# A two-block transformer kernel on one core: ring slots, rotations and first scores around its third attention reordered

## The reference, cut to what matters

```
q_l, k_l, v_l = jnp.split(h_lat @ w_in, 3, axis=-1)
q_l = apply_rope(q_l.reshape(B, S, DIFF_HEADS, 2, HEAD_DIM), cos, sin)
k_l = apply_rope(k_l.reshape(B, S, DIFF_HEADS, 2, HEAD_DIM), cos, sin)
k_c, v_c = jnp.split(h_ctx @ w_in[:, DIFF_QK_COLS:], 2, axis=-1)
...
s = jnp.einsum('bqhtd,bkhtd->bthqk', q, k).astype(jnp.float32) * HEAD_DIM ** -0.5
p = jax.nn.softmax(s, axis=-1)
a = (p[:, 0] - lam * p[:, 1]).astype(v.dtype)
o = jnp.einsum('bhqk,bkhe->bqhe', a, v)
```

## Time and profile before

| | |
|---|---|
| Median of 3 runs | 2924.38 us (2922.2 to 2927.43) |
| The profiled execution | 2922.9 us |
| Its span, first to last instruction | 2921.0 us |
| TensorE busy | 2822.2 us, 97% of the span |
| TensorE weight loads | 2314.3 us |
| DVE busy | 1386.3 us |
| ACT busy | 973.7 us |
| Mean granted TensorE clock | 0.985 of full |

### The profile page before, as it was taken

One profiled execution on the slowest core, in us unless ns is written; L12 is line 12 of the kernel. 1 busy time (PEld: TensorE's weight loads), 2 busy tenths in 40 slices (PEclk: granted clock), 3 DMA queues, 4 the chain that ended last, 5 costly groups with the idle time before them and its releaser, 6 DMA issues.

```text
span 2921.0 us, 43108 instructions
## 1 busy us (share of the span) xinstructions
PE 2822.2 (97%) x18438; PEld 2314.3 (79%) x18438; DVE 1386.3 (47%) x2449; ACT 973.7 (33%) x1565; POOL 63.1 (2%) x53
## 2 busy tenths in 40 slices
PE   7999999999999998999999999999998999999999
PEld 5876578888888887876778888887875788788887
DVE  3464553433233334325756646459478433443333
ACT  2144552422112224215635323342146322332221
POOL 2000000100000000000001001100000000000000
PEclk9999999999999999999999999999999999999999
DMA  6232101122332231220011333312220233222322
GB/s 263 87 102 77 36 12 48 58 102 105 116 127 101 103 107 30 65 65 22 1 58 59 101 102 96 99 59 66 87 84 23 65 94 101 87 86 85 104 96 85
DMA packets 67790, 238.53 MB, mean 82 GB/s; under 512 B 7440, under 2 KB 10640, under 8 KB 66960
## 3 DMA queue, kind: packets, MB, share of 16 engines
q1 hardware_dynamic: 67312, 234.20, 24.3%
q10 hardware_dynamic: 288, 1.57, 0.2%
HBM read 233.64 MB, written 2.10 MB: 81 GB/s over the span
## 4 chain that ended last, share of the span: by engine, by line
PE 91%; DVE 6%; ACT 2%; issue 1%; DMA 1%; SPq 0%; DVEq 0%; ACTq 0%
PE PSA L660 88%; PE PSA L966 2%; PE PSA L1246 1%; DVE stat L2988 1%; DVE WS L2213 1%; DMA Y<-in_early 1%; PE PSA L1556 0%; DVE Y L3001 0%; DVE HS L2383 0%; DVE PSA L2987 0%; ACT WS L1646 0%; ACT HS L1733 0%; DVE X L2321 0%; DVE X L2355 0%; ACT Y L1718 0%
## 5 line engine op out<-in xcount | busy, mean ns | idle before, releaser
L660 PE MATMUL PSA<-HS,WS 128*128 128x512 f32 (+1 forms) x6672 | 1349.3, 362 | 19.5 <-DVE HS L2383 12.8
L660 PEld LDWEIGHTS PSA<-HS,WS 128*128 128x128 f32 x6672 | 1124.7, 189 | 231.5 <-issue 30.5
L2213 DVE TENSOR_TENSOR WS<-W,WS 128x1024 fp32r<-128x1024 f32 (+2 forms) x318 | 364.3, 1147 | 610.2 <-ACT WS L1646 609.2
L1646 ACT ACTIVATE WS<-W 128x1024 fp32r<-128x1024 f32 (+2 forms) x318 | 314.1, 989 | 794.2 <-PE PSA L660 420.9
L660 PE MATMUL PSA<-YS,WS 128*128 128x512 f32 (+1 forms) x2232 | 470.2, 372 | 3.6 <-DVE YS L3026 3.6
L660 PEld LDWEIGHTS PSA<-YS,WS 128*128 128x128 f32 x2232 | 392.4, 189 | 79.1 <-DVE YS L3026 4.0
L660 PE MATMUL PSA<-Y 128*64 128x128 f32 (+9 forms) x2368 | 287.6, 345 | 16.6 <-ACT Y L1794 6.1
L660 PEld LDWEIGHTS PSA<-Y 128*64 128x64 f32 (+3 forms) x2368 | 178.5, 156 | 95.5 <-issue 69.2
L1630 ACT ACTIVATE Y<-PSA 128x512 f32<-128x512 f32 (+5 forms) x77 | 53.4, 699 | 243.0 <-PE PSA L660 242.9
L660 PE MATMUL PSA<-HS,YS 128*128 128x512 f32 (+1 forms) x696 | 129.1, 343 | 4.5 <-issue 4.1
L660 PEld LDWEIGHTS PSA<-HS,YS 128*128 128x128 f32 x696 | 108.5, 192 | 21.8 <-issue 7.3
(11 more groups left out here) (332 smaller groups left out, 2295.0 us busy)
## 6 DMA issues: line engine op xcount, KB each, us to landing
W<-in_weights SPq DMA_DIRECT2D x396, 512.0 KB, 3.6
Y<-in_early SPq DMA_DIRECT2D x4, 2048.0 KB, 18.6
W<-in_weights SPq DMA_DIRECT2D x24, 256.0 KB, 2.5
X<-in_x SPq DMA_DIRECT2D x4, 768.0 KB, 20.0
W<-in_weights SPq DMA_DIRECT2D x24, 128.0 KB, 2.1
Y<-in_ssm ACTq DMA_DIRECT2D x1, 1024.0 KB, 6.8
out<-X SPq DMA_DIRECT2D x1, 1024.0 KB, 4.6
C<-in_consts SPq DMA_DIRECT2D x1, 948.5 KB, 30.9
```

Of the source, the lines that this page charges most:

```text
L660: return pe.matmul(out, lhsT, rhs, start=first, stop=last)
L1646: act.activation(split_home(n)[:, 0, 0:f], W[:, c % W_RING, 0:f], ACT.Copy)\
L2213: tt(home[:, 1, 0:f], W[:, c % W_RING, 0:f], home[:, 0, 0:f].bitcast(F32), ALU.subtract)\
```

## The change

Four things, all of them in the order of instructions; no arithmetic is added or removed.

1. `first_tiles_of` (used at all five norms): the wait for the weights and the slot of each of the three tiles stands before that tile's first product, no longer before all three; the second tile goes to slot 2 and the third to slot 1. In DVE's table three residual adds stand earlier: at "ln2_0" tile 3's add at step 2 and not 3, at "ln2_1" at 4 and not 5, at "ffn_norm" at 5 and not 7.
2. Tiles of the third attention start in slot 0, not slot 3. The wait for slot 3 stands after tile 4. ACT copies the first three query tiles before it normalises range 1 of "ln2_0", and not after.
3. Rotations: one behind each of tiles 3 to 8, two behind tiles 9 and 10, one behind each from tile 11 on (that of the tile just before), and the last one behind the first value chunk. Value slots are taken one by one.
4. The two score matrices of unit 0 stand inside the last value chunk, behind its token tiles 3 and 4. The wait for the values' slots moves to unit 3. ACT loads the exponential's table before the last value copies, and copies the last value slot after unit 0's exponentials. DVE's three small operations on lambda follow the first two maxima, and the last weight chunk ("diff_in", 23) is released for splitting in unit 4, not before unit 0.

```diff
@@ first_tiles_of
-                for at, (key, chunk) in enumerate(jobs):
-                    pe.wait_ge(weights_split, s_index[chunk] + 1)
+                for at, (key, chunk) in zip((0, 2, 1), jobs):
                     ws.append(parts(chunk))
                     take(key, at)
-                    if turn(key) > 1:
-                        pe.wait_ge(psum_drained[slot(key)], turn(key) - 1)
...
                         for (key, chunk), w in zip(jobs, ws):
+                            if r == k == 0:
+                                pe.wait_ge(weights_split, s_index[chunk] + 1)
+                                if turn(key) > 1:
+                                    pe.wait_ge(psum_drained[slot(key)], turn(key) - 1)
@@ third attention, TensorE
-            back_to_ring()
+            skip_to_first_slot()
             for n in range(3, 16):
...
                 tile(jobs[n], ("diff_in", n), HT2, LAT if n < 8 else ALL)
-                rotate_diff(jobs[n - 3])
-            for n in range(13, 16):
-                rotate_diff(jobs[n])
+                if n == 4:
+                    for at in (4, 5):
+                        pe.wait_ge(psum_drained[at], given["slot", at])
+                for m in (n - 3,) if n < 9 else (2 * n - 12, 2 * n - 11) if n < 11 else (n - 1,):
+                    rotate_diff(jobs[m])
...
                     for t in range(6):
                         key = ("dv", g, t // 2)
+                        if c == 0 and t % 2 == 0:
+                            take(key)
+                            if turn(key) > 1:
+                                pe.wait_ge(psum_drained[slot(key)], turn(key) - 1)
...
+                        if g and c == 3 and t in (3, 4):
+                            if t == 3:
+                                for what in ("dq", "dk"):
+                                    pe.wait_ge(rope_done, value("rope_done", (what, 7)))
+                            diff_score(DIFF_UNITS[0], 0, t - 3)
...
+                    if g == c == 0:
+                        rotate_diff(jobs[15])
...
-                if n < len(units):
-                    diff_scores(units[n], n)
+                if 1 <= n < len(units):
+                    for t in range(2):
+                        diff_score(units[n], n, t)
+                if n == 3:
+                    for g in range(2):
+                        for j in range(3):
+                            pe.wait_ge(psum_drained[slot(("dv", g, j))], turn(("dv", g, j)))
@@ ACT
                 root_of(1)
+                if key == "ln2_0":
+                    for m in range(3):
+                        copy_out(("dq", m), QD[:, m, :], n=S, scale=HD ** -0.5)
                 for k in range(KD + 1):
                     scale_and_round(1, k)
...
+                if n == 0:
+                    keep_values(1, 2)
+                if n == 4:
+                    more_weights(("diff_in", 23))
@@ DVE
-                              {3: (("add", 3),)}),
+                              {2: (("add", 3),)}),
...
-                              {2: (("add", 2),), 5: (("add", 3),)}),
+                              {2: (("add", 2),), 4: (("add", 3),)}),
...
-                                 {2: (("add", 1),), 4: (("add", 2),), 7: (("add", 3),)})}[key]
+                                 {2: (("add", 1),), 4: (("add", 2),), 5: (("add", 3),)})}[key]
...
+                if n == 4:
+                    more_weights(("diff_in", 23))
```

More of the change, by code:

```diff
@@ L1194, in _, with diff_score @@
                 tile(jobs[n], ("diff_in", n), HT2, LAT if n < 8 else ALL)
-                rotate_diff(jobs[n - 3])
-            for n in range(13, 16):
-                rotate_diff(jobs[n])
+                if n == 4:
[3 more added lines that the diff above has]
+                    rotate_diff(jobs[m])
+            def diff_score(u, n, t):
+                _, h, i = u
+                key = (u, "scores", t)
+                take(key, t)
+                if turn(key) > 1:
+                    pe.wait_ge(psum_drained[slot(key)], turn(key) - 1)
+                r = slice(HD * t, HD * t + HD)
+                for c, j, nj in score_runs(u):
+                    ins = mm(PS[slot(key)][:, c * P:(c + nj) * P], QD[r, h, i * P:(i + 1) * P],
+                             KDf[r, h, j * P:(j + nj) * P], True, True)
+                ins.then_inc(psum_filled[slot(key)], 1)
             for g in range(2):
-                for j in range(3):
-                    take(("dv", g, j))
-                    if turn(("dv", g, j)) > 1:
-                        pe.wait_ge(psum_drained[slot(("dv", g, j))], turn(("dv", g, j)) - 1)
                 for c in range(4):
@@ L1219, in _ @@
                         w_last_job(("dv", g, 2), *chunk)
-            for g in range(2):
-                for j in range(3):
-                    pe.wait_ge(psum_drained[slot(("dv", g, j))], turn(("dv", g, j)))
-            for what in ("dq", "dk"):
-                pe.wait_ge(rope_done, value("rope_done", (what, 7)))
-            def diff_scores(u, n):
-                _, h, i = u
-                for t in range(2):
-                    key = (u, "scores", t)
-                    take(key, t)
-                    if turn(key) > 1:
-                        pe.wait_ge(psum_drained[slot(key)], turn(key) - 1)
-                    r = slice(HD * t, HD * t + HD)
-                    for c, j, nj in score_runs(u):
-                        ins = mm(PS[slot(key)][:, c * P:(c + nj) * P], QD[r, h, i * P:(i + 1) * P],
-                                 KDf[r, h, j * P:(j + nj) * P], True, True)
-                    ins.then_inc(psum_filled[slot(key)], 1)
+                    if g == c == 0:
+                        rotate_diff(jobs[15])
             def diff_transposes(u, n):
@@ L1909, in _, with keep_values @@
                 more_weights(("diff_in", 8 + m))
+            def keep_values(g, j):
+                key = ("dv", g, j)
+                act.wait_ge(psum_filled[slot(key)], turn(key))
+                act.activation(VD[:, 2 * j:2 * j + 2, g * S:(g + 1) * S],
+                               PS[slot(key)][:].rearrange("p (t c) -> p t c", t=2),
+                               ACT.Copy).then_inc(psum_drained[slot(key)], 1)
             for g in range(2):
@@ L1912, in _ @@
                     more_weights(("diff_in", 16 + 4 * g + c))
-                for j in range(3):
-                    key = ("dv", g, j)
-                    act.wait_ge(psum_filled[slot(key)], turn(key))
-                    act.activation(VD[:, 2 * j:2 * j + 2, g * S:(g + 1) * S],
-                                   PS[slot(key)][:].rearrange("p (t c) -> p t c", t=2),
-                                   ACT.Copy).then_inc(psum_drained[slot(key)], 1)
-                more_weights(("diff_in", 19 + 4 * g))
-            act.wait_ge(lambda_logs, value("lambda_logs"))
-            act.activation(stat[:, 34:36], stat[:, 32:34], ACT.Exp).then_inc(lambda_exps, one("lambda_exps"))
+                if g:
+                    act.wait_ge(lambda_logs, value("lambda_logs"))
+                    act.activation(stat[:, 34:36], stat[:, 32:34], ACT.Exp).then_inc(lambda_exps, one("lambda_exps"))
+                for j in range(2 if g else 3):
+                    keep_values(g, j)
+                if g == 0:
+                    more_weights(("diff_in", 19))
             def square_head(h):
@@ L2766, in _ @@
                                           negate=True).then_inc(row_max, one("row_max", (u, t)))
+                if n == 4:
+                    more_weights(("diff_in", 23))
+                if n == 0:
+                    dve.wait_ge(lambda_exps, value("lambda_exps"))
+                    link(tt(stat[:, 36:37], stat[:, 35:36], stat[:, 34:35], ALU.subtract))
+                    link(ts(stat[:, 36:37], stat[:, 36:37], -LAMBDA_INIT, None, ALU.add))
+                    link(ts(stat[:, 37:38], par("subln"), 1.0 - LAMBDA_INIT, None, ALU.mult))
                 if 1 <= n <= len(units):
```

9 lines of the change are left out of this document (3 added, 6 removed).

## The result

The changed kernel takes 2900.55 us (median; 2895.67 to 2903.02), the kernel before beside it 2923.29 (2920.4 to 2927.43). The ratio is 0.9916, with a 95% interval of 0.9904 to 0.9929: 0.71 to 0.96% faster. The forecast was 2897, the range 2889 to 2909. The profiled execution took 2902.61 us where that of before took 2922.9.

A forecast was written before the change was run, and what follows sets the result against it. TensorE was taken as the bound, busy 2822.2 of 2921.0 us, so only idle time and low clock could shrink. Terms 6.2 + 7.7 + 6.5 + 6.3 = 26.7 us off 2922.9 gave 2896.2, put at 2897; range 2889 to 2909.

The forecast's parts named there:

- A: Third attention's tile 3 in slot 0: a 4.12 us wait and 2.48 of clock saved, less 0.41; 6.2 us.
- at ln2_0 nothing is won: First tiles at ln2_0: ACT did not idle before the mean's copy, so its chain starts no earlier; 0 us.
- B: Third attention's rotations without lag: a 4.8 us wait ahead of the values and 2.95 of low clock saved; 7.7 us.
- C: Unit 0's scores inside the value products: 8.4 us won up to unit 4's scores, less 1.9; 6.5 us.
- R4: Rival: rotations without lag make TensorE wait at each of 13 tiles, so slower, 2929 us; chance 0.03.
- the split's price: Unit 4: DVE's split waits for ACT's rounding, TensorE's transposes wait 1.8 to 2 us; 1.9 taken off.
- Low clock again in the attention's first units: Sign that the prediction is wrong: slow-clock stretches reappear in the third attention's first units; no size given.
- D: First tiles slot by slot at five norms: 3.3 (ln2_1), 0.8 (ln1_0), 0.7 (ln1_1), 1.5 (ffn_norm); 6.3 us.
- R2: Rival: DVE and ACT set the attention's pace and take C back, C = 0, gain 20, 2903 us; chance 0.12.
- R1: Rival: the clock falls anyway, slow stretches only move; gain 16 us, 2907 us; chance 0.21.
- R3: Rival: splits don't hold ffn_norm back and unit 4's stall is hidden; gain 30.5, 2892 us; chance 0.12.
- R5: Rival: no change, the order moves but the same chains end last; 2924 us; chance 0.04.

The follow-up runs named there:

- A, B, D alone: Three kernels, each the kernel before with only the part of the change behind A, B or D: 2913.95, 2914.15 and 2917.64 us.
- scores behind the values (C undone): The changed kernel with unit 0's score products behind all value products again, ACT and DVE in their old order: 2903.02 us.
- D taken away: The changed kernel with the part on the first tiles undone at all five norms: 2910.21 us.
- halves together: The changed kernel with unit 0's two score halves together behind the fifth token tile of the last value chunk: 2900.95 us.
- split one unit later: The changed kernel with DVE's last weight split moved from unit 4 to unit 5, behind the combination: 2898.42 us.
- both edits: The changed kernel with split moved to unit 5 and unit 0's score halves together: 2895.29, 2898.19 us; third, ln2_0's first tiles as before: 2894.09 us.

## Why the forecast was near, point by point

**A was right, and 6.2 was within what the runs gave**: 7.2 in the profiled pair, 6.0 against the two others. The forecast put tile 3's 24 products at the 6.05 us of the next tile; with the clock up they take 5.60, so more came back from the clock than 2.48. The 0.41 put on the statistics was right as a delay: they start 20.5 us after the row of 15 matmuls, before 20.1. What the forecast did not see is the low clock behind it: 18 products took 5.74 us instead of 4.37. The term "at ln2_0 nothing is won" should have read 2.0 lost in this pair. Over all profiles the fall stands in 7 of 8 with the new order; with the old one, in 2 of 5 behind the statistics and in 1 of 5 behind the first tiles' wait.

**B was right**: 7.7 forecast, 7.7 alone, and 7.3 in the pair, where the missing 0.4 is the part of C's two breaks that wasn't taken off. Rival R4 had nothing for it: no rotation has a bracket.

**C was the step that failed**. The forecast was 8.4 - 1.9 = 6.5, and the changed kernel got 0. Of the 8.4 up to unit 4's scores 3.6 came: they start 17.1 us after the values' end, where 20.7 stood and 12.3 were forecast. And the split's price was 3.6 and not 1.9. Low clock again in the attention's first units was named as a sign that the prediction is wrong, and it came.

| kernel | values' end to unit 6's scores |
|---|---|
| before | 28.8 us |
| A, B, D alone | 28.9, 30.3, 28.8 |
| scores behind the values (C undone) | 28.3 |
| changed, twice | 28.9, 28.9 |
| D taken away | 28.8 |
| halves together | 28.1 |
| split one unit later | 25.3 |
| both edits, three times | 22.3, 22.3, 22.3 |

Three things took what is missing. First, "one after the other they took 3.81 at half clock, so 1.9 at full clock" misread the row. The 3.81 was the pair at low clock, its halves side by side; parted, the two breaks cost 2.97 from start to start and 3.4 in all. The same misreading is in "unit 1's first half ends after 0.95": unit 1's maxima begin 1.66 us after its scores (1325.87 - 1324.21), so unit 2's scores start 3.7 us after the end and not 2.8. These two take 2.0 of the 4.8 missing up to unit 4's scores. Second, behind unit 2's wait of 1.58 the clock fell and the scores of units 2 and 3 ran at 0.50. From unit 2's to unit 4's scores it took 10.4 us, 8.1 where the clock stayed up: 2.3. The rest, 0.5, isn't traced to a row. The stretches of the changed kernel and of the one with both edits:

```profile
1324.00:1328.00 4.00, 2.42 (x11) 1.00 0.00 0
1328.00:1332.00 4.00, 4.00 (x11) 0.64 0.00 0
1332.00:1336.00 4.00, 4.00 (x13) 0.50 0.00 0
...
1346.00:1350.00 4.00, 3.48 (x18) 0.57 0.44 129
```

```profile
1326.00:1330.00 4.00, 2.65 (x10) 1.00 0.00 0
1330.00:1334.00 4.00, 3.24 (x14) 1.00 0.00 0
1334.00:1338.00 4.00, 3.82 (x21) 1.00 0.00 0
```

Third, the split's stall came as forecast, 2.12 us for "1.8 to 2", but it too was followed by low clock (0.57 from 1346 us), which made it 3.6. With all three away the gain at this place is 28.8 - 22.3 = 6.5 us, by chance just the forecast.

The two edits add. From unit 4's to unit 6's scores the kernels with the split in unit 4 took 11.8 or 11.9 us (changed twice, D taken away, halves together) and those with it in unit 5 took 8.3 (four profiles): 3.5 us for the split. Up to unit 4's scores the four kernels with the pair have the same attention, and from tile 4 on they took 182.0 us three times and 184.2 once, where the changed kernel took 185.4. The 184.2 is the profile of the pair alone, with low clock behind its wait of 1.32. So the pair gives 3.4 us where the clock stays up and gave 1.2 where it fell; moving the split cannot be what kept it up, since that comes later. Why it fell in one of four isn't shown.

Rival R2 named the right number (C = 0) with half of the reason. What it said of the split came: VectorE, behind ACT's rounding, took back in unit 4 what had been won ahead of it. But the attention's engines did not take back more, or the split moved could not have brought 3.6 us, and both edits 6.8 that still stand at ln1_1.

**D was right in sum, but not at each place.** In the profiled pair ln2_1's nine products have no bracket and take 1.42 us, ln1_1's 1.52, the final norm's 1.65, as forecast; at the final norm a wait of 0.85 for the reciprocal behind the weight splits came later, the very thing named for taking 1.5 and not 2.9. At ln1_0 the wait went too: the statistics start 1.1 us earlier after the products ahead. But their own wait of 2.08 stayed, the clock fell behind it in this profile, and that took 1.5 back. Over all profiles it fell there in 6 of 9 with the new order and in 2 of 4 with the old one. D taken away from the changed kernel cost 9.7 us, and D alone gave 5.5. One place accounts for part of it: the wait of 2.9 at the final norm was followed by nine products of 1.31 us in the profile of before and of 2.26 in the three later profiles that have it. At ln2_1 it is the other way round: behind the wait of 1.97 the nine products took 2.14 in the earlier trace rows and 1.81, 1.31 and 1.31 in the three later profiles that have it, so the 0.83 and 0.5 put on the clock there were more than the other three lose. The forecast took one execution for the rule. How much of the 9.7 that makes isn't settled.

**Rival R1 was partly so.** The clock's losses moved as well as went: two new low stretches stand behind the statistics at ln1_0 and ln2_0. But TensorE's busy time fell by 6.1 us for the same matmuls, so most of what A and B promised from the clock came.

**The balance**, in us of the profiled pair: forecast 26.7, span shorter by 20.6, so 6.1 missing. C lacks 6.5, ln1_0 and the noise ahead of it 2.0 (0.8 forecast, 1.2 lost), ln2_0 1.6 (2.0 lost, 0.4 forecast) and B 0.4, which belongs to C's breaks. Against that A gave 0.6 more, the stretch to ln1_1 1.5 more (2.2 for 0.7) and the rest to the end 2.3 more (7.1 for 4.8); of the last two some came without any term, by the clock alone in code that the change doesn't touch. So it is in part luck that the total came near: 2900.55 is nearer to R2's 2903 than to 2897, and without the 4.4 us beyond the terms it would have been about 2905. R3, which needed a hidden stall in unit 4, and R5, no change, did not come.

## What to carry to other kernels

When work is slipped into another stage, look at how its matmuls overlap each other where they stand now: two halves that use different rows of the array cost one when they are neighbours, and two when they are parted. Price a wait of TensorE as its length and as what the clock takes behind it; here an edit worth 2.1 us of waiting gave 3.6. Before calling two edits more than their sum, compare stretches that only one of them can touch: here the pair gave 1.2 or 3.4 us by whether the clock fell. Read the clock from several executions before a term is built on it, and judge parts of a change by a segment of the trace, since the whole time of this kernel moves by 7 us from run to run.

## What the runs showed of the hardware

- Half of a score pair (4 matmuls of 64 rows) alone among 128-row products took 1.48 and 1.49 us from its start to the next product's; the pair (8 matmuls) took 1.50 in the same place. By the whole stretch two parted halves cost 3.4 us and the pair 1.7. What the change of mode costs in this is not separated. An estimate: four rotations of 512 columns and 128 rows take 3.60 us, by which the 768 columns of a half take 1.35, so at most some 0.35 of the 1.7 is left for going in and out. The Trainium skill, TensorEngine Tiling (Tiling Modes, Key Properties), says beside it that different tiles can run matmuls in parallel; the trace agrees with that sentence, and no run here shows what its other one, on the drain, costs.
- The granted clock is not set by the wait alone. The same chain of waits (0.57 and 1.32 us) was followed by low clock in one profile (scores of 3.08 and 3.60 us) and by full clock in three (2.44 and 2.44), and the wait of 2.9 us at the final norm by full clock in one and low clock in three. The Trainium skill, TensorE: Matmul & The Clock Gate (Part 1), has a window that runs freely; by that rule such pairs are to be expected, and the traces show them, though no run here shows the window itself.
- Executions of one kernel differ with the mean granted clock: those of the kernel before took 2920.08 us at 0.985 and 2928.07 at 0.982.
